# Prompt attention: the first layer's modulation products inside a tile's projection, rope gains in the rope tables, rope copies in one instruction

## The reference

```python
def ada_modulation(c, w, b):
    m = jax.nn.silu(c) @ w + b            # (9 rows) x (1024 x 6144), once per layer
    return jnp.split(m, 6, axis=-1)

q = (cq @ w_q_up).reshape(B, T, N_HEADS, QK_NOPE_DIM + QK_ROPE_DIM)   # 8 heads of 128 + 64
qn = rmsnorm(q[..., :QK_NOPE_DIM], g_qn)
qr = rope(rmsnorm(q[..., QK_NOPE_DIM:], g_qr), pos)

def rope(x, pos):                         # x1, x2: the halves of 64
    return jnp.concatenate([x1 * cos - x2 * sin, x2 * cos + x1 * sin], axis=-1)
```

## Time and profile before

| what | value |
|---|---|
| median of 3 runs | 2835.72 us |
| the profiled execution, its own time | 2833.41 us |
| its span, first to last instruction | 2831.7 us |
| mean granted TensorE clock | 0.99 |
| PE busy / PEld busy | 96% / 86% |
| DVE / ACT / POOL busy | 65% / 40% / 31% |
| projection parts in the span, about | 144 to 184, 242 to 282, 341 to 381, 438 to 477 us |

### The profile page before, as it was taken

The page is one execution under the profiler, slowest core; times in us unless marked ns, Lnnn a source line. Parts: engine busy times, 40 slices in busy tenths (PEclk is TensorE's granted clock), DMA queues, the critical chain, the costliest instruction groups (busy, mean ns, idle before and its releaser), DMA issues.

```text
span 2831.7 us, 46606 instructions
## 1 busy us (share of the span) xinstructions
PE 2731.1 (96%) x15902; PEld 2448.9 (86%) x15902; DVE 1841.1 (65%) x3078; ACT 1141.9 (40%) x2375; POOL 874.3 (31%) x939
## 2 busy tenths in 40 slices
PE   7989999799999999999999999999999999999998
PEld 4978877789997889898989897888899999999997
DVE  4577787655565766767676775233667676767675
ACT  3355555445562343434343423223234343434331
POOL 1122011146661022525252552000003434343344
PEclk9999999999999999999999999999999999999999
DMA  6244434322244311111111158124421111111118
GB/s 236 79 161 146 145 110 147 124 76 74 67 158 129 105 45 44 44 44 46 43 52 39 56 136 239 30 83 144 154 83 45 44 44 44 44 44 44 44 59 149
DMA packets 123517, 255.11 MB, mean 90 GB/s; under 512 B 16036, under 2 KB 66116, under 8 KB 120072
## 3 DMA queue, kind: packets, MB, share of 16 engines
q1 hardware_dynamic: 117304, 231.20, 24.6%
q0 software_dynamic: 6096, 22.35, 4.0%
HBM read 213.39 MB, written 40.12 MB: 90 GB/s over the span
## 4 chain that ended last, share of the span: by engine, by line
PE 66%; DVE 1%; SPq 1%; issue 0%; DMA 0%; POOL 0%; ACT 0%; POOLq 0%; DVEq 0%; ACTq 0%
PE psum L112 21%; PE psum L110 21%; PE psum L111 21%; PE psum L3141 1%; PE psum L3282 1%; PE psum L3256 0%; DMA gate_wu_raw<-in_cm_w_in 0%; PE psum L3293 0%; SPq L2297 0%; DMA half_m<-scratch_mixT 0%; DVE half_out L2894 0%; DVE half_w_lo L2763 0%; DVE gate_x L3026 0%; DVE gate_x L3029 0%; SPq L2292 0%
## 5 line engine op out<-in xcount | busy, mean ns | idle before, releaser
L110 PE MATMUL psum<-half_hT_hi,half_w_hi 128*128 128x384 f32 x1536 | 513.7, 334 | 0.0
L112 PE MATMUL psum<-half_hT_hi,half_w_lo 128*128 128x384 f32 x1536 | 513.5, 334 | 0.0
L111 PE MATMUL psum<-half_hT_lo,half_w_hi 128*128 128x384 f32 x1536 | 513.3, 334 | 0.0
L2645 POOL TENSOR_TENSOR half_acc<-half_acc,half_upd 128x512 f32<-128x512 f32 x312 | 423.0, 1374 | 33.6 <-ACT half_upd L2414 29.4
L112 PE MATMUL psum<-half_w_hi,half_s_lo 128*128 128x512 f32 x1040 | 405.7, 390 | 0.0
L111 PE MATMUL psum<-half_w_lo,half_s_hi 128*128 128x512 f32 x1040 | 405.7, 390 | 0.0
L110 PE MATMUL psum<-half_w_hi,half_s_hi 128*128 128x512 f32 x1040 | 405.3, 390 | 0.0
L2861 DVE TENSOR_TENSOR half_acc<-half_acc,psum 128x512 f32<-128x512 f32 x416 | 279.3, 681 | 81.5 <-PE psum L112 81.4
L2397 ACT ACTIVATE half_s_raw<-psum 128x384 f32<-128x384 f32 (+2 forms) x256 | 97.7, 407 | 560.9 <-PE psum L112 560.9
L111 PEld LDWEIGHTS psum<-half_hT_lo,half_w_hi 128*128 128x128 f32 x1536 | 288.4, 188 | 1.2
L110 PEld LDWEIGHTS psum<-half_hT_hi,half_w_hi 128*128 128x128 f32 x1536 | 288.4, 188 | 1.2
(11 more groups left out here) (405 smaller groups left out, 5749.3 us busy)
## 6 DMA issues: line engine op xcount, KB each, us to landing
half_w_raw<-in_w SPq DMA_DIRECT2D x64, 512.0 KB, 4.2
half_w_raw<-in_w SPq DMA_DIRECT2D x128, 256.0 KB, 3.4
patt_mod_w<-in_ada_w_ffn SPq DMA_DIRECT2D x32, 768.0 KB
patt_mod_w<-in_ada_w_att SPq DMA_DIRECT2D x16, 1024.0 KB, 5.0
half_m<-scratch_mixT SPq DMA_DIRECT2D x18, 512.0 KB, 5.1
satt_lT_raw<-in_cacheT SPq DMA_DIRECT2D x32, 256.0 KB, 3.0
satt_l_raw<-in_cache SPq DMA_DIRECT2D x32, 256.0 KB, 3.2
half_w_raw<-in_w_o SPq DMA_DIRECT2D x16, 512.0 KB, 5.2
```

What stands on the lines that cost most here:

```text
L110: pe.matmul(out, a_hi, b_hi, start=first, stop=False)
L111: pe.matmul(out, a_hi, b_lo, start=False, stop=False)
L112: return pe.matmul(out, a_lo, b_hi, start=False, stop=last)
L2645: pool.tensor_tensor(part, part, a.upd[n % UPDS][:], ALU.add).then_inc(a.added, 1)
```

## The change

It has three parts.

1. A modulation product of the first layer stands in `proj(t)`, between the tile's query products and its key products, and goes into the last quarter (columns 384 to 511) of the query bank of that tile. `mod_tile` sets the tiles: 3, 5, 7 and 9 in the first pair (9 stands for the old place in `tokT(7)`, bank 7), and 1, 3, 5 and 7 in the other pairs. DVE takes a product up at the start of `tile(t)` of the same tile.
2. SP loads weights 0 and table 0 of the first pair ahead of the two attention constants, and those of the next pair behind the store of attention group g = 2. In a pair, weights 1 come before the `mod1` weights.
3. The rope gain is multiplied into the cosine and sine tables once, ahead of the pairs. `tile(t)` then takes rope's three products from PSUM, adds once into `qr`, and one 256-wide multiply by `rs` writes both copies. It is eight instructions; the `dve_step` waits have a 128-wide instruction between the producer and the wait.

```diff
--- before.py
+++ after.py
@@ -633,7 +633,14 @@
 
         mod_w = ph.sb("mod_w", [P, HK, 4 * ATT_N])
         mod_tab, mod = ph.sb("mod_tab", [P, 3, ATT_N]), ph.sb("mod", [P, ATT_N])
-        mod_psum = psum[:, 7, 3 * P:]
+
+        def mod_tile(p, i):
+
+            return 2 * i + 1 if p > 0 else 2 * i + 3
+
+        def mod_psum(t):
+            return psum[:, 2 * (t % 3) if t < T else 7, 3 * P:]
+
         mod1_w, mod1_in = ahead.mod1_w, ahead.mod1_in
         mod1_tab, mod1 = ph.sb("mod1_tab", [P, 3, FFN_N]), ph.sb("mod1", [P, FFN_N])
         mod1_psum = [psum[:, bank, 2 * P:2 * P + FFN_N] for bank in (7, 1, 1, 6)]
@@ -706,10 +713,8 @@
                         load_mod1_tab(p, i + 1)
 
                 def pair(p, last):
-                    load_mod_w(p, 0)
-                    load_mod_tab(p, 0)
+                    load_mod_w(p, 1)
                     load_mod1_w(p, 1)
-                    load_mod_w(p, 1)
                     load_mod_w(p, 2)
                     store_mod1(p, 0)
                     store_mod(p, 0)
@@ -726,6 +731,9 @@
                             store_mod1(p, 1)
                         if g == 1:
                             load_mod1_w(p, 3)
+                        if g == 2 and not last:
+                            load_mod_w(p, 4)
+                            load_mod_tab(p, 2)
                         if g == 3:
                             store_mod1(p, 2)
                         if g == 3 and last:
@@ -740,6 +748,8 @@
                 sp.sem_inc(mod_stored, 64)
                 sp.sem_inc(mod1_stored, 64)
                 load_mod1_tab(0, 0)
+                load_mod_w(0, 0)
+                load_mod_tab(0, 0)
                 for dst, src in ((ident_bf, "ident_bf"), (mask, "mask")):
                     sp.dma_start(dst[:], io[src]).then_inc(const_in, 16)
                 with sp.Fori(0, PAIRS - 1) as p:
@@ -869,20 +879,29 @@
                     b, s, HW, hr = 2 * (t % 3), t % 2, DN + DR, DR // 2
                     dve.wait_ge(r_ready, p * T + (2 + t + 1))
                     dve.wait_ge(tokT_raw, p * T + (t + 1))
-                    for j in range(2):
-                        q = psum[:, b, j * HW:(j + 1) * HW]
-                        dve.scalar_tensor_tensor(qr[:, j, :], q[:, DN:], rs[:, s, 2 + j:3 + j], g_qr[:],
+                    q = psum[:, b, 0:2 * HW].rearrange("p (j x) -> p j x", j=2)
+
+                    for i in range(4):
+                        if mod_tile(p, i) == t:
+                            read_mod(p, i, step)
+
+                    def nope(j):
+                        dve.scalar_tensor_tensor(q_tok[:, s, j, :], q[:, j, 0:DN], rs[:, s, j:j + 1], gg[:],
                                                  ALU.mult, ALU.mult)
-                        last = dve.scalar_tensor_tensor(q_tok[:, s, j, :], q[:, 0:DN], rs[:, s, j:j + 1], gg[:],
-                                                        ALU.mult, ALU.mult)
-                    step.run(last)
+
                     cos_t = cos[:, t, :].unsqueeze(1).to_broadcast([P, 2, DR])
                     sin_t = sin[:, t, :].unsqueeze(1).to_broadcast([P, 2, DR])
-                    dve.tensor_tensor(qr_cos[:], qr[:], cos_t, ALU.mult)
-                    dve.tensor_tensor(qr_sin[:, :, 0:hr], qr[:, :, hr:], sin_t[:, :, 0:hr], ALU.mult)
-                    step.run(dve.tensor_tensor(qr_sin[:, :, hr:], qr[:, :, 0:hr], sin_t[:, :, hr:], ALU.mult))
-                    for i in range(2):
-                        dve.tensor_tensor(q_tok[:, s, 2:4, i * DR:(i + 1) * DR], qr_cos[:], qr_sin[:], ALU.add)
+                    dve.tensor_tensor(qr_cos[:], q[:, :, DN:], cos_t, ALU.mult)
+                    dve.tensor_tensor(qr_sin[:, :, 0:hr], q[:, :, DN + hr:], sin_t[:, :, 0:hr], ALU.mult)
+                    step.then(dve.tensor_tensor(qr_sin[:, :, hr:], q[:, :, DN:DN + hr], sin_t[:, :, hr:], ALU.mult))
+                    nope(0)
+                    step.done()
+                    step.then(dve.tensor_tensor(qr[:], qr_cos[:], qr_sin[:], ALU.add))
+                    nope(1)
+                    step.done()
+                    dve.tensor_tensor(q_tok[:, s, 2:4, :].rearrange("p j (i x) -> p j i x", i=2),
+                                      qr[:].unsqueeze(2).to_broadcast([P, 2, 2, DR]),
+                                      rs[:, s, 2:4].unsqueeze(2).unsqueeze(3).to_broadcast([P, 2, 2, DR]), ALU.mult)
                     dve.wait_ge(ktok_ready, p * T + (t + 1))
                     dve.tensor_tensor(v_lo[:, t, :], psum[:, b + 1, 2 * DN:], f(v_hi[:, t, :]), ALU.subtract
                                       ).then_inc(tok_ready, 1)
@@ -892,17 +911,22 @@
                     dve.wait_ge(tokT_hi_ready, p * T + (t + 1))
                     if t == 0:
                         read_mod1(p, 0)
-                    if t % 4 == 1:
-                        dve.wait_ge(mod_tab_in, p * 32 + 16 * (t // 4 + 1))
-                        dve.wait_ge(mod_stored, p * 128 + 64 * (t // 4 + 1))
-                        step.run(dve.tensor_tensor(mod[:], mod_psum, mod_tab[:, BIAS, :], ALU.add))
-                    if t % 4 == 3:
-                        mod_finish(dve, step, mod[:], mod_psum, mod[:], mod_tab).then_inc(mod_ready, 1)
+                    if t == T - 1 and mod_tile(p, 3) > t:
+                        read_mod(p, 3, step)
                     q = psum[:, b, :].rearrange("p (k n) -> p k n", k=4)
                     dve.tensor_tensor(qT_lo[:, :, toks], q[:, 0:2, :], f(qT_hi[:, 0:2, toks]), ALU.subtract)
                     dve.tensor_tensor(qT_hi[DR:, 2:4, toks], q[DR:, 2:4, :], f(qT_hi[DR:, 2:4, toks]), ALU.subtract)
                     dve.tensor_tensor(kT_lo[:, :, toks], psum[:, b + 1, 0:2 * P].rearrange("p (k n) -> p k n", k=2),
                                       f(kT_hi[:, :, toks]), ALU.subtract).then_inc(tokT_ready, 1)
+
+                def read_mod(p, i, step):
+                    products = mod_psum(mod_tile(p, i))
+                    if i % 2 == 0:
+                        dve.wait_ge(mod_tab_in, p * 32 + 16 * (i // 2 + 1))
+                        dve.wait_ge(mod_stored, p * 128 + 64 * (i // 2 + 1))
+                        step.run(dve.tensor_tensor(mod[:], products, mod_tab[:, BIAS, :], ALU.add))
+                    else:
+                        mod_finish(dve, step, mod[:], products, mod[:], mod_tab).then_inc(mod_ready, 1)
 
                 def read_mod1(p, i):
                     dve.wait_ge(mod1_used, p * 4 + (1 + i + 1))
@@ -974,6 +998,12 @@
                 dve.sem_inc(tokT_ready, 2)
                 dve.sem_inc(pT_ready, 2)
                 dve.wait_ge(ahead.gains_in, 16 * 5)
+                hr = DR // 2
+                for table, part, gain in ((cos, slice(0, DR), slice(0, DR)), (sin, slice(0, hr), slice(hr, DR)),
+                                          (sin, slice(hr, DR), slice(0, hr))):
+                    row = g_qr[:, gain].unsqueeze(1)
+                    dve.tensor_tensor(table[:, :, part], table[:, :, part],
+                                      row.to_broadcast([P, TT, part.stop - part.start]), ALU.mult)
                 dve.tensor_tensor(gg[:], g_qn[:], g_kn[:], ALU.mult).then_inc(gg_ready, 1)
                 dve.wait_ge(gg_ready, 1)
                 for p in range(PAIRS):
@@ -983,7 +1013,14 @@
             def _(pe):
                 def proj(p, t):
                     pe.wait_ge(tok_ready, p * T + (t + 1))
-                    ahead.project(pe, p, t, cqT, ckvT, psum)
+                    ahead.project(pe, p, t, cqT, ckvT, psum, lambda: modulation(p, t))
+
+                def modulation(p, t):
+                    for i in range(4):
+                        if mod_tile(p, i) == t:
+                            pe.wait_ge(mod_w_in, p * 64 + 16 * (i + 1))
+                            mod_products(pe, mod_psum(t), c_silu, mod_w, (i % 2) * HK, HK, ATT_N, True, True
+                                         ).then_inc(mod_w_used, 1)
 
                 def tokT(p, t):
                     b, s = 6, t % 2
@@ -991,11 +1028,8 @@
                     if t == 0:
                         pe.wait_ge(o_ready, p * GN + 2)
                         mod1_step(p, 0)
-                    if t % 2 == 1:
-                        i = t // 2
-                        pe.wait_ge(mod_w_in, p * 64 + 16 * (i + 1))
-                        mod_products(pe, mod_psum, c_silu, mod_w, (i % 2) * HK, HK, ATT_N, True, True
-                                     ).then_inc(mod_w_used, 1)
+                    if t == T - 1:
+                        modulation(p, t + 2)
                     pe.wait_ge(tok_ready, p * T + (3 + t + 1))
                     for k in range(4):
                         pe.transpose(psum[:, b, k * P:(k + 1) * P], q_tok[:, s, k, :], ident[:])
@@ -1144,13 +1178,14 @@
         dve.wait_ge(self.w_hi_ready, p * 2 + (i + 1))
         dve.tensor_tensor(lo[:], raw[:], f(hi[:]), ALU.subtract).then_inc(self.w_ready, 1)
 
-    def project(self, pe, p, t, cqT, ckvT, psum):
```

(2 more changed lines are left out.)

## The result

The changed kernel takes **2852.41 us** (median of 4 runs, 2850.57 to 2857.08) where the kernel before, beside it, took 2835.59 us: ratio 1.0061, 95% interval 1.0044 to 1.0078, **+16.8 us**. The forecast was 2846.2 us (+10.5), with a range that ended at 2850. The sign was right; the size was not, and the time lies outside the range.

A forecast was written before the change was run, and what follows sets the result against it. The prediction took PE's chain as the bound, with a projection loop over two tiles and late loads deciding. Pair terms of -0.4, 3.95, 3.95 and 3.0 gave +10.5 us, median 2846.2 us; range 2836 to 2850.

The forecast's parts named there:

- Loop and product's place: Projection's two-tile loop: 8.37 us, 9.38 with a product; moving the product within it counts nothing in mid-pair.
- rival 1: Table and weights land before they are wanted; only earlier products cost, +1.3 us per pair, +3.5, 2839.2 us; chance 0.25.
- DVE's tile: DVE's rope block falls from 2.03 to 1.55 us, PSUM reads cost nothing; it saves only where DVE is late.
- SP's line: Pairs two to four: loads behind SP's stores come late; DVE waits 3.3 us for table 1, PE 2.7 for weights 3.
- Landing of weights 3: Weights 3 from issue to landing: between 5.0 and 6.4 us, middle 5.7 taken; bounds 0.7 us either way in three pairs.
- rival 3: Engines carrying the table begin the weights only once it has landed: 6.4 us in three pairs, 2848.3 us; chance 0.20.
- What follows product 3: Second pair from product 3 to tile 7's splits: L902 of tile 7 at 288.26, before 284.31, so +3.95 us.
- The sum: All four pairs: -0.4 + 3.95 + 3.95 + 3.0 = +10.5 us, median 2846.2 us.
- First pair: Weights 0's wait of 1.40 us goes or shrinks, but the product delays ACT: -0.5 to +0.5, taken as -0.4 us.
- The products fill PE's waits: PE is bound by DVE's read-out, a product ahead is free: at most 9.8 + 1.4 us go, 2824.5 us; chance 0.10.

The follow-up runs named there:

- the first pair's rounds: The changed kernel with all four pairs using the first pair's tiles (3, 5, 7 and the old place in the transposes of tile 7); 2837.56 us, ratio 1.0016.
- loads first: The changed kernel with SP issuing table 1 and weights 3 earlier, ahead of stores they had stood behind; 2838.11 us, ratio 1.0017 to the kernel before.
- 24 transposes: The changed kernel with PE making 24 identity transposes ahead of the wait for weights 3 in pairs two to four; 2852.15 us, ratio 1.0060.

## Why the prediction was right and wrong

- **Loop and product's place.** Inside the loop right: 9.59 us measured, 9.38 forecast, 9.54 before. "in the middle of a pair I count nothing" holds only there. At the loop's ends the place costs: 7.5 us between the two kernels that differ in it alone, loads in time in both. In the sum it was covered by the late loads from tile 5 on; of rival 1 I had +3.5, and its kernel measures +4.5.
- **DVE's tile.** Right: 1.52 us, no loss from PSUM. That it saves only where DVE is late is right too; the runs put about 4 us on it in the change.
- **SP's line.** The distances hold (4.69 us from store to table, 0.85 to the weights; 4.66 and 0.7 forecast). The start was 1.0 us too late in my sum: "2 x 1.01 later" counted product 0 ahead of tileT(1), but it is made ahead of tile 0's transposes and is paid in the rest before.
- **Landing of weights 3.** The step "so I take the middle, 5.7" failed: 6.5, 6.8, 7.0 us. The upper bound, rival 3's mechanism, was the truth or short of it. In the second pair this and the early start cancel: product 3 was forecast for 274.66 and starts at 274.66. The waits are 3.30, 3.76 and 2.42 us, where I had 2.7, 2.7 and, with SP 0.95 us faster, about 1.8.
- **What follows product 3.** Here the step that failed most. The chain from product 3 on (275.67, v_hi 277.26, L902 280.39, maxima 285.56, L902 of tile 7 288.26) takes the upper clock for granted: the half clock behind a wait is in no term. Measured: L917 at 282.62, maxima at 287.75, L917 of tile 7 at 290.28, each 2.0 to 2.2 us later, which is the 2.08 us of the half clock. Without it tile 7's splits would be 3.9 us later than before (290.28 - 284.31 - 2.08), and +3.95 was forecast.
- **The sum.** Forecast -0.4, 3.95, 3.95, 3.0; measured +0.1, +5.9, +7.5, +3.6, so 6.6 us short. Split into parts and rests, the parts grow by 0.5, 6.5, 6.4 and 5.1 us. In pairs two to four that is 7.0 us more than forecast: 5.2 are the half clock behind product 3, and the later landings are in the remainder. The rests, which I had at nothing, change by -0.4, -0.6, +1.1 and -1.5 us. Each of the first three has gained product 0 (about 1 us). But in the execution before, the clock also falls at the first softmax products of the first, second and fourth pair, and those rests are about 1.5 us longer for it (66.7 and 66.6 against 65.1 in the third; 63.5 against 62.0 in the fourth of the kernel with the rope part alone, where the clock stayed up); the falls in the change's rests cost 0.3 us at most. So the fourth pair's +3.6 is near the forecast 3.0 by luck: its part alone grew by 5.1.
- **First pair.** -0.4 forecast, +0.1 measured, of two large parts: 1.85 us gained in the part by the earlier weights 0 and the rope, 2.3 lost in it by the products' place (33.63 against 31.30, with 3.4 us at half clock in it).
- **Rivals.** "The products fill PE's waits" fell: the waits for DVE's read-out moved from the products to the transposes and grew, from 9.8 + 5.5 to 20.3 us. "Loads in time" did not happen, and gives +4.5 when made to. The range failed because its upper end was little more than the landing's bound, with the clock as certain.

## What to carry to other kernels

Before moving work earlier, move what feeds it: the change took the products two rounds ahead and left their loads behind stores that nobody waits for, and that was 12 of its 17 us. Place a small piece of work so that it stands behind, not ahead of, what the next engine waits for; the same 1.08 us product, ahead of tile 7's key products instead of behind them, brought the transposes of tile 6 about 1.2 us later. And when a forecast puts a wait of some us on TensorE, its upper bound should price the next products at half clock too. Compare single traces phase by phase: here the code behind prompt attention, the same in all kernels, took 2291.4 to 2298.2 us in the profiled executions, a spread larger than most of the effects.

## What was not expected of the hardware

- Behind every wait of 2.4 us or more ahead of product 3, nine of nine (two executions of the change and one with rope undone), the granted clock fell to 0.50 and stayed there for 3.4 to 6.8 us. A product then takes up to 1.94 us instead of 1.08. The length of the wait does not decide it alone: ahead of tile 6's transposes, 2.44 us are followed by half clock in all four pairs with the first pair's rounds and in two of four with loads first, and with weights 3 ahead of table 1 the clock stayed up through 3.04 us and fell at 2.82. A shorter one is not safe either: with 24 transposes it fell at 2.00 us. No run here tells what decides.
- Weights 3 took 4.9 to 5.7 us to land with the table's 192 KB behind them, and 6.3 to 7.9 us in all 24 loads of six traces in which the table went 0.5 to 0.9 us ahead of them.
